# Loading x and w_ada ahead of the states' matrices, and setting up the states behind the first norm

## The chip, the cores and the metric

The kernel runs on one core of a Trainium2 chip. The metric is the device time of one execution in microseconds, the median of several runs. A core has five engines with instruction queues of their own: TensorE (PE, matrix products into eight PSUM banks), VectorE (DVE), ScalarE (ACT), GpSimd (POOL) and SyncE (SP, which here only issues DMA transfers). They wait for each other through semaphores.

## The reference, cut to what matters

One block of a hybrid model is followed by a second one of another kind; 512 tokens, 1024 features, float32. Only the beginning of the first block matters here:

```python
c_act = silu(c)
mod = c_act @ w_ada + b_ada              # six parts of 1024 columns: sh1, sc1, g1, sh2, sc2, g2
h = standardize(x) * (1 + sc1) + sh1     # the first norm
proj = h @ w_in + b_in                   # split into xm, om, ip, fp, us, ga, gb
xc = silu(causal_dwconv(xm))             # then q, k of the mLSTM heads, and v = xm
ys = gelu(s5_ssm(us, ...))               # 32 groups of 16 channels with 64 complex states each
```

In the state space model (the "states"), a small setup comes first: `dt = exp(log_dt)`, the decay `a = exp(lam * dt)` by magnitude, cosine and sine, and `b_bar = z * b` with complex `z = (a - 1) / lam`. The kernel handles eight tokens at a time: it needs the powers 0 to 8 of `a`, multiplied with c (`G5`) and with `b_bar` (`T5`), a Toeplitz matrix of the eight first responses, and a scan over 64 chunks.

## The kernel before, in words

**Weights.** All large products are float32 made of three passes: a weight block is loaded raw (512 KB, SyncE), ScalarE copies it, rounded, to `w_hi` (L1165), GpSimd subtracts to get the rest `w_lo` (L2369), and TensorE multiplies hi by hi, hi by lo and lo by hi. The blocks stand in one list (`STREAM`) that goes round through 3 raw slots, 3 `w_hi` and 3 `w_lo` slots. A raw slot is loaded again when `w_lo` of the block three before is made; a `w_hi` slot is written again when the product of the block three before has ended. `feature` (L620) takes a block of 128 output features: 24 matmuls of 128x512 (L614 to L616). `feature_pair` (L639) takes two blocks, tile by tile of h, so that it can start with the first tiles (L650 to L652). The order is us 0 to 3, xm 0 to 7, om 0 to 7, gate, gb 0 to 7, then the rest.

**The opening.** SyncE's queue issues in this order: four constants (`cols`, `ident`, `causal`, `iota`), six small transfers of the states' matrices b and c, x (2 MB), eight transfers of w_ada (1 MB each, two rows of 128 in each; parts 0 and 1, the shift and the scale). Ahead of the last two it waits until VectorE and TensorE have read b and c, which lie where these two land. Then come the weight blocks. VectorE makes the setup of the states, takes the row statistics of x (L1666), the root, and then multiplies the rows of w_ada with c and adds them up (`ada_add`, L1771 and L1773). TensorE takes three of the sixteen rows over itself (`first_columns`, L718: 5 and 7 of part 0, 7 of part 1), folds VectorE's sum over the partitions (`other_columns`, L724), and `ada_columns` (L1810) writes `mod`. ScalarE normalises x to `xn1` (L1181), TensorE turns it to eight feature tiles (`turn_h1`, L707), and ScalarE and VectorE make `h_hi` and `h_lo` out of each (`modulated`, L1200 and L1204; `modulated_low`, L1779 and L1661). A product can't start before these.

**PSUM banks.** `take` (L592) goes round a ring of banks; a bank has to be free before TensorE writes it, and TensorE's queue waits for that in order. In the opening the ring is `[4, 5, 6, 1, 2, 3, 0, 7]`: c's two transpositions take 4 and 5, part 0 takes 6, tiles 0 to 2 of h take 1, 2, 3, part 1 takes 0, and tiles 3 to 7 take 7, 4, 5, 6 and 4. The last one waits for `h_lo` of tile 4.

**The states beside the blocks.** Behind the first norm VectorE makes `G5` (L1915 to L1925, `times_powers`), the padded b (`pads`, L1931 and L1935), `T5`, and the phases of the tables (L1938 to L1946). TensorE's part stands between blocks, by a list (n counts xm 0 to 7 and om 0 to 7):

```python
s5_after = {2: [s5_kernel], 4: [lambda: s5_turn(0), lambda: s5_turn(1)], 6: [s5_inputs], 12: [s5_outputs]}
```

`s5_kernel` (L770) needs `G5` and the pads, `s5_turn` (L782) transposes each half of `T5` when it is set, `s5_inputs` (L787) needs the turned `T5` and us, `s5_outputs` (L801) needs the scans. ScalarE has a list of its own with the same steps: behind the turns it makes sine tables from the phases (L1250), behind the outputs it copies them and issues eight transfers to DRAM (L1260), and it has SiLU for the convolution of xm (`conv_out`, L1262). GpSimd sets the Toeplitz matrix to zero (L2377) behind `w_lo` of us 3.

Of the kernel before, what the change touches and what calls it, by code (L numbers as in the profile page):

```python
# [12 lines left out]
P = 128  # L13
# [142 lines left out]
def build(nc, io, out):  # L156
    with ExitStack() as ctx:
# [86 lines left out]
        T5 = [part(flat_xc, 2048 * i, NST, LC, S5G) for i in range(2)]  # L244
        ada_place = [(0, 2 * i, part(buf, 2 * (i % 2) * D, 2, D)) for i, buf in enumerate((flat_xc, flat_xc, flat_xm, flat_xm))]
        ada_place += [(1, 2 * i, part(buf, at + 2 * (i % 2) * D, 2, D)) for i, (buf, at) in enumerate(((usys, 0), (usys, 0), (s5a, 8704), (s5a, 8704)))]

        ADA_PE = ((5, 7), (7,))
# [229 lines left out]
        const_in = signal("const_in", 4, 16)  # L478
        s5_in = signal("s5_in", 6, 16)
# [3 lines left out]
        x_in = signal("x_in", 1, 16)  # L483
# [226 lines left out]
        def first_columns(part_):  # L710
# [3 lines left out]
            for kk in ADA_PE[part_]:  # L714
                n = 4 * part_ + kk // 2
                pe.wait_ge(*ada_in[n].all)
                for f in range(KD):
                    te.matmul(ps[:, f:f + 1], ada_place[n][2][:, kk % 2, f * P:(f + 1) * P], c_act[:, kk:kk + 1], start=(kk == ADA_PE[part_][0] and f == 0), stop=False)  # L718
# [21 lines left out]
        def tensor():  # L740
            pe.wait_ge(*const_in.all)
            pe.wait_ge(*s5_in.all)
            ring["misc"], turn["misc"] = [4, 5, 6, 1, 2, 3, 0, 7], 7
            for i in range(2):
                transpose(("c5", i), [c_nat[i][:, J, :, :].rearrange("p a b -> p (a b)") for J in range(4)], c_turned[2 * i + 1])
# [74 lines left out]
            s5_after = {2: [s5_kernel], 4: [lambda: s5_turn(0), lambda: s5_turn(1)], 6: [s5_inputs], 12: [s5_outputs]}  # L820
# [389 lines left out]
        def scalar():  # L1210
# [1326 lines left out]
```

## Time and profile before

| | |
|---|---|
| median of 3 runs | 1668.94 us (1664.17 to 1670.81) |
| the profiled execution | 1668.08 us, its span 1666.3 us |
| TensorE busy | 1598.5 us (96%) |
| VectorE, ScalarE, GpSimd busy | 768.3, 611.9, 618.3 us |
| first product of a weight block | at 52.03 us |

The profile page has the busy time of each engine and the chain of work that ended last, followed back from the last instruction. Its timeline lists instructions by start and duration; an entry with a count merges several. A bracket tells how long the engine sat idle before, and what released it. Overlap of a few tenths between neighbouring instructions of one engine is pipelining.

### The profile page before, as it was taken

The page shows a single profiled execution, that of the slowest core. Times are in us where ns is not written, and L with a number is a line of the kernel's source. Part 1 is how long each engine was busy: PE and PEld are TensorE (multiplying, and loading weights), DVE is VectorE, ACT ScalarE, POOL GpSimd, SP SyncE. Part 2 cuts the span into 40 slices and gives each one's busy share as a digit, 9 for nine tenths or more (in the row PEclk, how much of TensorE's full clock was granted, in tenths as well). Part 3 has the DMA queues.
Part 4 walks back from the last instruction along what each step waited for, and adds up shares of the span by engine and source line. Part 5 has one row for each costly group of instructions (what it writes and reads, how often), then busy time and mean ns, then how long its engine had stood idle before and what let it go on. Part 6 is the DMA issues. An engine that isn't in the chain of part 4 may idle for free.

```text
span 1666.3 us, 18583 instructions
## 1 busy us (share of the span) xinstructions
PE 1598.5 (96%) x7532; PEld 1298.5 (78%) x7532; DVE 768.3 (46%) x1344; ACT 611.9 (37%) x887; POOL 618.3 (37%) x266
## 2 busy tenths in 40 slices
PE   4899999989998999999999999999999999999998
PEld 4788867778887888878887888678877788888886
DVE  7879223556667444123306799751441621012103
ACT  3443464343425333123322434582442343124312
POOL 0443222224344444444454464003323344444442
PEclk9999999999999999999999999999999999999999
DMA  9393431238634354333332432002212233233322
GB/s 318 96 152 110 114 95 46 69 114 288 228 108 132 109 147 146 95 88 90 101 114 88 146 102 89 26 1 76 77 51 76 84 106 101 89 89 101 101 89 76
DMA packets 221669, 180.26 MB, mean 108 GB/s; under 512 B 24200, under 2 KB 184328, under 8 KB 221456
## 3 DMA queue, kind: packets, MB, share of 16 engines
q1 hardware_dynamic: 212368, 166.48, 34.6%
q10 hardware_dynamic: 9216, 12.60, 2.4%
q8 instruction: 59, 0.97, 0.2%
q14 instruction: 26, 0.21, 0.0%
HBM read 172.49 MB, written 6.55 MB: 107 GB/s over the span
## 4 chain that ended last, share of the span: by engine, by line
PE 78%; DVE 11%; ACT 3%; POOL 2%; issue 2%; DMA 2%; ACTq 0%; SPq 0%; DVEq 0%; POOLq 0%
PE bank L614 14%; PE bank L615 14%; PE bank L616 14%; PE bank L671 7%; PE bank L669 7%; PE bank L670 7%; DVE bank L2197 5%; PE bank L707 2%; POOL w_lo L2369 2%; DMA raw<-in_w_in 1%; PE bank L1041 1%; PE bank L1012 1%; PE bank L908 1%; PE bank L691 1%; PE bank L1098 1%
## 5 line engine op out<-in xcount | busy, mean ns | idle before, releaser
L2369 POOL TENSOR_TENSOR w_lo<-raw,w_hi 128x1024 fp32r<-128x1024 f32 (+1 forms) x246 | 595.5, 2425 | 1003.4 <-ACT w_hi L1165 1003.1
L1165 ACT ACTIVATE w_hi<-raw 128x1024 fp32r<-128x1024 f32 (+1 forms) x246 | 257.7, 1050 | 350.0 <-PE bank L671 276.6
L614 PE MATMUL bank<-h_hi,w_hi 128*128 128x512 f32 x936 | 369.8, 395 | 8.2 <-POOL w_lo L2369 6.1
L615 PE MATMUL bank<-h_lo,w_hi 128*128 128x512 f32 x936 | 366.7, 392 | 0.0
L616 PE MATMUL bank<-h_hi,w_lo 128*128 128x512 f32 x936 | 366.7, 392 | 0.0
L614 PEld LDWEIGHTS bank<-h_hi,w_hi 128*128 128x128 f32 x936 | 177.2, 189 | 50.6 <-issue 8.7
L616 PEld LDWEIGHTS bank<-h_hi,w_lo 128*128 128x128 f32 x936 | 177.0, 189 | 37.3
L615 PEld LDWEIGHTS bank<-h_lo,w_hi 128*128 128x128 f32 x936 | 177.1, 189 | 37.0 <-issue 0.7
L2197 DVE SCALAR_TENSOR_TENSOR bank<-att_area,cols,bank 128x512 f32<-128x512 f32 x116 | 87.6, 755 | 3.9
L671 PE MATMUL bank<-w_hi,u_lo 128*128 128x512 f32 x224 | 88.6, 396 | 0.0
L670 PE MATMUL bank<-w_lo,u_hi 128*128 128x512 f32 x224 | 88.6, 396 | 0.0
L669 PE MATMUL bank<-w_hi,u_hi 128*128 128x512 f32 x224 | 88.6, 396 | 0.0
L1734 DVE SCALAR_TENSOR_TENSOR x_tok<-bank,sm,x_tok 128x512 f32<-128x512 f32 x16 | 12.0, 749 | 154.9 <-PE bank L671 81.6
L2322 DVE TENSOR_TENSOR rel<-rel 128x512 f32<-128x512 f32 x32 | 30.7, 958 | 95.7 <-ACT rel L1638 95.7
L1753 DVE TENSOR_TENSOR bank<-bank,grow 128x512 f32<-128x512 f32 x24 | 16.6, 692 | 106.3 <-PE bank L693 54.3
L669 PE MATMUL bank<-w_hi,h_hi 128*128 128x512 f32 x160 | 63.8, 399 | 0.0
L671 PE MATMUL bank<-w_hi,h_lo 128*128 128x512 f32 x160 | 63.1, 394 | 0.0
L670 PE MATMUL bank<-w_lo,h_hi 128*128 128x512 f32 x160 | 62.8, 393 | 0.0
L671 PE MATMUL bank<-w_hi,act_lo 128*128 128x512 f32 x136 | 53.8, 396 | 0.0
L670 PE MATMUL bank<-w_lo,act_hi 128*128 128x512 f32 x136 | 53.8, 396 | 0.0
L669 PE MATMUL bank<-w_hi,act_hi 128*128 128x512 f32 x136 | 53.8, 396 | 0.0
L2143 DVE TENSOR_SCALAR cv_t<-tmp_f,cols 128x512 f32<-128x512 f32 x22 | 14.1, 640 | 82.7 <-ACT tmp_f L1476 82.7
(429 smaller groups left out, 2686.3 us busy)
## 6 DMA issues: line engine op xcount, KB each, us to landing
raw<-in_w_in SPq DMA_DIRECT2D x57, 512.0 KB, 4.0
raw<-in_w_ffn_up SPq DMA_DIRECT2D x44, 512.0 KB, 3.8
raw<-in_w_up SPq DMA_DIRECT2D x32, 512.0 KB, 4.0
raw<-in_w_down SPq DMA_DIRECT2D x32, 512.0 KB, 3.8
ada_ring<-in_w_ada SPq DMA_DIRECT2D x24, 512.0 KB, 5.6
raw<-in_w_ffn_down SPq DMA_DIRECT2D x20, 512.0 KB, 3.7
raw<-in_w_s_glu SPq DMA_DIRECT2D x16, 256.0 KB, 3.0
raw<-in_w_mlstm_down SPq DMA_DIRECT2D x8, 512.0 KB, 5.9
```

The lines of the kernel that those rows point to most:

```text
L614: te.matmul(ps, wv[0][:, i, :], rh, start=(i == 0), stop=False)
L615: te.matmul(ps, wv[0][:, i, :], rl, start=False, stop=False)
L616: last = te.matmul(ps, wv[1][:, i, :], rh, start=False, stop=(i == kt - 1))
L669: te.matmul(bank[b][:, :], ah, wv[0][:, i, :], start=first, stop=False)
L670: te.matmul(bank[b][:, :], ah, wv[1][:, i, :], start=False, stop=False)
L671: last = te.matmul(bank[b][:, :], al, wv[0][:, i, :], start=False, stop=final)
L691: te.matmul(bank[b][:, :], ah, wv[0][:, i, :], start=False, stop=False)
L707: last = te.transpose(ps[0:s_.shape[1], i * P:i * P + s_.shape[0]], s_, ident[0:s_.shape[0], 0:s_.shape[0]])
L1165: sc.activation(W_HI[SLOT[key]][:, 0:n], raw[:, RAW_SLOT[key], 0:n], ACT.Copy).then_inc(*hi_set.up(key))
L2197: dve.settle().scalar_tensor_tensor(acc, upad[:, f, j:j + S], w_, acc, ALU.mult, ALU.add).then_inc(*dve.step())
L2322: ve.tensor_tensor(sq, rl, rl, ALU.mult).then_inc(*u_sq.up(m))
L2369: gp_.tensor_tensor(W_LO[s_][:, 0:n], raw[:, RAW_SLOT[key], 0:n], W_HI[s_][:, 0:n].bitcast(F32), ALU.subtract).then_inc(*lo_made.up(key))
```

## The change

SyncE issues x behind three constants, in two halves, then w_ada, then three weight blocks; the states' matrices and `causal` follow once part 1's columns are folded. w_ada goes in nine transfers, the last two of one row of 128 each, and TensorE's own rows are now 1 and 3 of part 0 and 1 of part 1. VectorE starts with the norm, and the setup of the states stands behind `modulated_low`; ScalarE's exponent and sine for it stand behind `modulated`. TensorE transposes c behind the first pair of blocks. The ring of banks is another one. `s5_kernel`, `s5_turn` and `s5_inputs` come two blocks later, `s5_outputs` one, and the wait for the Toeplitz matrix's transfers with them; GpSimd's memset comes behind xm 3.

```diff
-        ada_place += [(1, 2 * i, part(buf, at + 2 * (i % 2) * D, 2, D)) for i, (buf, at) in enumerate(((usys, 0), (usys, 0), (s5a, 8704), (s5a, 8704)))]
-        ADA_PE = ((5, 7), (7,))
+        ada_place += [(1, 2 * i, part(buf, at, 2, D)) for i, (buf, at) in enumerate(((usys, 0), (usys, 2 * D), (s5a, 8704)))]
+        ada_place += [(1, 6 + i, part(s5a, 8704 + (2 + i) * D, 1, D)) for i in range(2)]
+        ADA_PE = ((1, 3), (1,))
...
         def tensor():
             pe.wait_ge(*const_in.all)
-            pe.wait_ge(*s5_in.all)
-            ring["misc"], turn["misc"] = [4, 5, 6, 1, 2, 3, 0, 7], 7
-            for i in range(2):
-                transpose(("c5", i), [c_nat[i][:, J, :, :].rearrange("p a b -> p (a b)") for J in range(4)], c_turned[2 * i + 1])
+            ring["misc"], turn["misc"] = [4, 1, 2, 5, 6, 3, 0, 7], 7
...
             first_columns(0)
+            for f in range(4):
+                turn_h1(f)
             other_columns(0)
-            for f in range(3):
-                turn_h1(f)
             first_columns(1)
-            turn_h1(3)
+            turn_h1(4)
             other_columns(1)
-            for f in range(4, 7):
-                turn_h1(f)
-            turn["misc"] = 7
+            turn_h1(5)
+            turn_h1(6)
+            turn["misc"] = 4
             turn_h1(7)
...
             feature_pair([("us", 0), ("us", 1)], h_hi, h_lo, h1_ready, [us_out[0], us_out[1]])
+            pe.wait_ge(*s5_in.all)
+            for i in range(2):
+                transpose(("c5", i), [c_nat[i][:, J, :, :].rearrange("p a b -> p (a b)") for J in range(4)], c_turned[2 * i + 1])
...
-            s5_after = {2: [s5_kernel], 4: [lambda: s5_turn(0), lambda: s5_turn(1)], 6: [s5_inputs], 12: [s5_outputs]}
+            s5_after = {4: [s5_kernel], 6: [lambda: s5_turn(0), lambda: s5_turn(1)], 8: [s5_inputs], 13: [s5_outputs]}
...
         def scalar():
-            act.wait_ge(*s5_dve["pow"])
-            sc.activation(E9, E9, ACT.Exp).then_inc(*s5_act.up("pow"))
-            act.wait_ge(*s5_dve["cs"])
-            sc.activation(pw5[:, 0:288], pw5[:, 288:576], ACT.Sin, scale=SIN_SCALE).then_inc(*s5_act.up("cs"))
...
                 modulated("h1", f, mod[:, KD + f:KD + f + 1], mod[:, f:f + 1], h1_sv, h1_dv, h1_hi)
+            act.wait_ge(*s5_dve["pow"])
+            sc.activation(E9, E9, ACT.Exp).then_inc(*s5_act.up("pow"))
+            act.wait_ge(*s5_dve["cs"])
+            sc.activation(pw5[:, 0:288], pw5[:, 288:576], ACT.Sin, scale=SIN_SCALE).then_inc(*s5_act.up("cs"))
...
-            s5_after = {2: [s5_kernel], 4: [lambda: s5_turn(0), lambda: s5_turn(1), s5_tables], 9: [lambda: conv_out(0, 2)], 12: [s5_outputs], 13: [lambda: conv_out(2, 4)], 14: [lambda: conv_out(4, 6)], 15: [lambda: conv_out(6, 8)]}
+            s5_after = {4: [s5_kernel], 6: [lambda: s5_turn(0), lambda: s5_turn(1), s5_tables], 10: [lambda: conv_out(0, 2)], 13: [s5_outputs, lambda: conv_out(2, 4)], 14: [lambda: conv_out(4, 6)], 15: [lambda: conv_out(6, 8)]}
...
         def vector():
+            for i in range(2):
+                dve.wait_ge(*x_in[i].all)
+                row_stats(2 * i, 2, x_tok)
+            row_variance("x", 0, TT, 0, LN_EPS, False)
+            row_inverse("x", 0, TT, 0, shift=True)
+            dve.wait_ge(*c_set.all)
+            for p_ in range(2):
+                for kk in ada_dve(p_):
+                    n, rows_ = ada_rows_at[p_, kk]
+                    ada_add(p_, kk, rows_, ada_in[n].all)
+                    if (p_, kk) == (1, 6):
+                        ada_columns(0, 0, 0.0)
+            ada_columns(1, KD, 1.0)
+            dve.wait_ge(*mod_set[1])
+            for f in range(0, KD, 2):
+                modulated_low("h1", f, KD, 0, h1_dv, h1_hi, h1_lo)
...
             dve.wait_ge(*turned["h1", KD - 1])
+            dve.wait_ge(*c_turned[3])
             times_powers(G5, c5, LC + 1, -1, g5_set)
...
         def gpsimd():
             gp_.memset(ones[:, :], 1.0).then_inc(*ones_set.up())
-            pool_low_to(INDEX["us", 3])
-            pool.wait_ge(*ada_sum[1])
-            pool.wait_ge(*ada_col[1])
+            pool_low_to(INDEX["xm", 3])
+            pool.wait_ge(*b5_set.all)
+            pool.wait_ge(*turned["c5", 1])
             gp_.memset(toep, 0.0).then_inc(*toep_zero.up())
...
         def sync():
+            def s5_matrices():
+
+                sp.wait_ge(*ada_col[1])
+                for i, nm in enumerate(("s5_b_re", "s5_b_im")):
+                    sy.dma_start((b_re, b_im)[i], io[nm][0].rearrange("g p c -> (g p) c").rearrange("(j p) c -> p j c", p=P)).then_inc(*s5_in.up(i))
+                for i, nm in enumerate(("s5_c_re", "s5_c_im")):
+                    for d_ in range(2):
+                        sy.dma_start(c_nat[i][:, :, d_, :], io[nm][0].rearrange("g c p -> (g c) p").rearrange("(j p) s -> p j s", p=P)).then_inc(*s5_in.up(2 + 2 * i + d_))
+                sy.dma_start(causal[:, :], io["causal"]).then_inc(*s5_in.up(6))
...
+            for i in range(2):
+                sy.dma_start(x_tok[:, 2 * i:2 * i + 2, :], io["x"][0, 2 * i * P:2 * (i + 1) * P].rearrange("(t p) d -> p t d", p=P)).then_inc(*x_in[i].up())
             for n, (p_, k0, place_) in enumerate(ada_place):
-                if n == len(ada_place) - 2:
-                    sp.wait_ge(*turned["c5", 1])
-                    sp.wait_ge(*b5_set.all)
...
             for r_, (key, parts) in enumerate(STREAM):
+                if r_ == NRAW:
+                    s5_matrices()
...
-                if key == ("om", 0):
+                if key == ("om", 2):
                     sp.wait_ge(*k_rows_out.all)
                     sp.wait_ge(*toep_zero.all)
```

## Rows read from the trace of the kernel before

**Rows 1.** The page: TensorE's busy time, and the chain that ended last.
```profile
PE 1598.5 (96%) x7532; PEld 1298.5 (78%) x7532; DVE 768.3 (46%) x1344; ACT 611.9 (37%) x887; POOL 618.3 (37%) x266
...
PE 78%; DVE 11%; ACT 3%; POOL 2%; issue 2%; DMA 2%; ACTq 0%; SPq 0%; DVEq 0%; POOLq 0%
```

**Rows 2.** TensorE's waits, 0 to 330 us: us in total, times, longest.
```profile
PE bank L718 <- DMA xmT<-in_w_ada: 12.5, 1, 12.5
PE bank L707 <- DMA s5a<-in_s_c_im: 9.8, 1, 9.8
PE bank L707 <- DVE h_lo L1661: 3.7, 1, 3.7
PE bank L614 <- POOL w_lo L2369: 3.3, 3, 1.9
```

**Rows 3.** Timeline, 0 to 56 us: start, duration, engine, line, operation.
```profile
2.59 0.43 SPq L2403 DMA_DIRECT2D s5a<-in_s_b_re  x1
...
6.30 0.18 DVE L1829 TENSOR_TENSOR s5a<-cols,s5a 128x16 f32<-128x16 f32 x1 [1.38 <-ACT s5a L1213]
...
7.20 0.51 SPq L2407 DMA_DIRECT2D x_tok<-in_x  x1
...
14.97 1.77 DVE L1887 COPY s5a<-bank 64x256 f32<-64x256 f32 x4
...
16.77 4.85 DVE L1666 BATCH_NORM_STATS2 stats<-x_tok 128x6 f32<-128x512 f32 x8
...
38.73 1.27 DVE L1773 SCALAR_TENSOR_TENSOR scr<-s5a,sm,scr 128x1024 f32<-128x1024 f32 x1
38.82 1.06 ACT L1165 ACTIVATE w_hi<-raw 128x1024 fp32r<-128x1024 f32 x1 [10.42 <-DMA raw<-in_w_in]
...
41.46 3.41 PE L724 MATMUL bank<-ones,scr 128*128 128x1 f32 x16
...
44.91 0.17 DVE L1810 SCALAR_TENSOR_TENSOR mod<-bank,cols 128x8 f32<-128x8 f32 x1 [4.91 <-PE bank L724]
...
46.52 1.29 DVE L1661 SCALAR_TENSOR_TENSOR h_lo<-bank,h_hi 128x512 fp32r<-128x512 f32 x2 [0.59 <-ACT h_hi L1204]
...
51.26 1.12 PE L707 MATMUL bank<-ident,s5a 128*128 128x128 f32 x4 [3.73 <-DVE h_lo L1661]
...
52.03 0.78 PE L650 MATMUL bank<-h_hi,w_hi 128*128 128x512 f32 x1
```

**Rows 4.** The tile x_tok: its transfer.
```profile
DMA to landing us min/median/max: 9.2/9.2/9.2
```

**Rows 5.** A stretch: busy time of each engine, granted clock, DMA share, GB/s.
```profile
10.00:20.00 10.00, 1.76 (x8) 1.36 (x7) 9.46 (x31) 1.26 (x1) 0.00 (x0) 1.00 1.02 404
```

**Rows 6.** VectorE's and GpSimd's timelines, 50 to 330 us.
```profile
80.72 4.37 DVE L1915 TENSOR_TENSOR xcT<-s5a 128x2048 f32<-128x2048 f32 x1
85.01 2.28 DVE L1918 TENSOR_TENSOR s5a<-s5a 128x2048 f32<-128x2048 f32 x1
...
67.63 4.25 POOL L2369 TENSOR_TENSOR w_lo<-raw,w_hi 128x1024 fp32r<-128x1024 f32 x1 [20.70 <-ACT w_hi L1165]
...
80.53 2.41 POOL L2369 TENSOR_TENSOR w_lo<-raw,w_hi 128x1024 fp32r<-128x1024 f32 x1 [0.31 <-ACT w_hi L1165]
...
192.49 0.96 POOL L2381 MEMSET rows<- 128x1024 f32 x1
```

**Rows 7.** The tile usys, 190 to 197 us: duration ns min/median/max, starts.
```profile
L1989 DVE SCALAR_TENSOR_TENSOR usys<-usys,cols x4: 737/738/752, 192.3 to 194.4; 128x512 f32<-128x512 f32 x4
```

**Rows 8.** The chain that ended last, in order of time.
```profile
107.59 3.49 PE bank L707 x32
...
182.84 1.07 ACT w_hi L1165
...
199.25 1.75 PE bank L707 x16
```

**Rows 9.** TensorE in stretches of 2 us: busy, granted clock, DMA.
```profile
186.00:188.00 2.00, 1.52 (x4) 0.67 0.16 40
188.00:190.00 2.00, 2.00 (x6) 0.50 0.94 300
```

More of the change, by code:

```diff
@@ L245, in build @@
         ada_place = [(0, 2 * i, part(buf, 2 * (i % 2) * D, 2, D)) for i, buf in enumerate((flat_xc, flat_xc, flat_xm, flat_xm))]
-        ada_place += [(1, 2 * i, part(buf, at + 2 * (i % 2) * D, 2, D)) for i, (buf, at) in enumerate(((usys, 0), (usys, 0), (s5a, 8704), (s5a, 8704)))]
-        ADA_PE = ((5, 7), (7,))
+        ada_place += [(1, 2 * i, part(buf, at, 2, D)) for i, (buf, at) in enumerate(((usys, 0), (usys, 2 * D), (s5a, 8704)))]
+        ada_place += [(1, 6 + i, part(s5a, 8704 + (2 + i) * D, 1, D)) for i in range(2)]
+        ada_rows_at = {(p_, k0 + i): (n, place_[:, i, :]) for n, (p_, k0, place_) in enumerate(ada_place) for i in range(place_.shape[1])}
+        ADA_PE = ((1, 3), (1,))
         ada_acc = [grow, scr[:, 0:2, :].rearrange("p a b -> p (a b)")]
@@ L477, in build @@
         TTC = [(c, t) for t in range(TT) for c in range(2)]
-        const_in = signal("const_in", 4, 16)
-        s5_in = signal("s5_in", 6, 16)
+        const_in = signal("const_in", 3, 16)
+        s5_in = signal("s5_in", 7, 16)
         us_rows_out, us_chunks_in = signal("us_rows_out", US, 16), signal("us_chunks_in", LC, 16)
@@ L482, in build @@
         ys_rows_out, ys_in = signal("ys_rows_out", LC, 16), signal("ys_in", 1, 16)
-        x_in = signal("x_in", 1, 16)
+        x_in = [signal(f"x{i}_in", 1, 16) for i in range(2)]
         ada_in = [signal(f"ada{i}_in", 1, 16) for i in range(len(ada_place))]
@@ L714, in first_columns @@
             for kk in ADA_PE[part_]:
-                n = 4 * part_ + kk // 2
+                n, rows_ = ada_rows_at[part_, kk]
                 pe.wait_ge(*ada_in[n].all)
                 for f in range(KD):
-                    te.matmul(ps[:, f:f + 1], ada_place[n][2][:, kk % 2, f * P:(f + 1) * P], c_act[:, kk:kk + 1], start=(kk == ADA_PE[part_][0] and f == 0), stop=False)
+                    te.matmul(ps[:, f:f + 1], rows_[:, f * P:(f + 1) * P], c_act[:, kk:kk + 1], start=(kk == ADA_PE[part_][0] and f == 0), stop=False)
         def other_columns(part_):
@@ L1887, in vector @@
                     ve.tensor_copy(c5[i][gs, :, :], src[gs, :, g, :]).then_inc(*c_turned.up(2 * i + g))
-            dve.wait_ge(*x_in.all)
-            row_stats(0, TT, x_tok)
-            row_variance("x", 0, TT, 0, LN_EPS, False)
-            row_inverse("x", 0, TT, 0, shift=True)
-            dve.wait_ge(*c_set.all)
-            for p_ in range(2):
-                for kk in ada_dve(p_):
-                    n = 4 * p_ + kk // 2
-                    ada_add(p_, kk, ada_place[n][2][:, kk % 2, :], ada_in[n].all)
-                    if (p_, kk) == (1, 5):
-                        ada_columns(0, 0, 0.0)
-            ada_columns(1, KD, 1.0)
-            dve.wait_ge(*mod_set[1])
-            for f in range(0, KD, 2):
-                modulated_low("h1", f, KD, 0, h1_dv, h1_hi, h1_lo)
             def times_powers(dst, x, n, signs, done):
@@ L2398, in sync @@
         def sync():
[L2399 to L2407 removed]
+            def s5_matrices():
[6 more added lines that the diff above has]
+                sy.dma_start(causal[:, :], io["causal"]).then_inc(*s5_in.up(6))
+            for i, (dst, nm) in enumerate(((cols, "cols"), (ident, "ident"))):
+                sy.dma_start(dst[:, :], io[nm]).then_inc(*const_in.up(i))
+            sy.dma_start(iota, io["iota"][:, 0:NC]).then_inc(*const_in.up(2))
+            for i in range(2):
+                sy.dma_start(x_tok[:, 2 * i:2 * i + 2, :], io["x"][0, 2 * i * P:2 * (i + 1) * P].rearrange("(t p) d -> p t d", p=P)).then_inc(*x_in[i].up())
             for n, (p_, k0, place_) in enumerate(ada_place):
[L2409 to L2411 removed]
                 rows_ = slice(k0 * P, (k0 + place_.shape[1]) * P)
```

8 lines of the change are left out of this document (removed).

## The prediction

> **What bounds the kernel now.** I read the page first. TensorE is busy for 96% of the span and holds 78% of the chain that ended last [rows 1], so what can be gained is time in which it has no matmul. Next came TensorE's own waits over the first 330 us [rows 2]: 12.5 and 9.8 us fall ahead of the first real product, 3.7 on `h_lo`, 3.3 on `w_lo`. Then I followed the timeline up to that product [rows 3]. The six transfers for the states are issued from 2.59 us, x only at 7.20. x takes 9.2 us to land [rows 4], so until 16.4. VectorE starts its statistics at 16.77 and from there has no gap until its last row of w_ada at 38.73 + 1.27 = 40.0. TensorE folds that sum (41.46 to 44.87), `mod` is set at 45.08, and the first product starts at 52.03. It could have begun when `h_lo` of tiles 0 and 1 was there, at 46.52 + 1.29 = 47.8; it stood behind the transposition of tile 7, which waited until 51.26 for the bank of tile 4. After that products follow each other, and no later wait in that list is for anything that keeps its own date (a transfer issued early, say). A start g earlier is a gain of g unless the states' work turns up late.
>
> **The first norm.** Four transfers instead of ten stand ahead of x; its first half goes out at 2.1 us. The DMA moves 404 GB/s at full rate [rows 5], 2.6 us per MB. x's 2 MB need 5.2 us, so before they began to flow at 11.2; the small packets of the states had the time ahead of it. The constants land 2.4 us after their issue, so I put x's flow at 4, its halves at 6.5 and 9.1, and the eight MB of w_ada at 11.7, 14.3, ... 27.2, 29.8. Latest case: x at 10.5. VectorE: statistics cost 4.85 / 8 = 0.61 each [rows 3], four of them behind the second half, to 11.6; variance and root take 2.0, as before, so the first row at 13.6. Rows cost 0.75 and then 1.33 each; six, then seven. They now run into the DMA: part 0 ends at 22.2, part 1 can't pass its second transfer before 24.6, and ends at 32.8. TensorE's share, columns of rows 1 and 3 and then row 1, is early. Folding takes 3.5 + 0.2: `mod` at 36.5 instead of 45.08, 8.6 earlier (7 to 9.5). ScalarE's three `w_hi` must be ahead of that: before, the first raw block was there at 38.82 [rows 3], 1.9 us behind w_ada's end, the others at 40.6 and 42.1; so now 31.7, 33.5 and 35.0, and the last copy ends at 36.1.
>
> **The banks.** Tile 7 now takes part 1's bank, free once `mod` is set. TensorE turns tiles 5 to 7 until 39.1, and `h_lo` of tile 1 is there 2.7 us after `mod`, at 39.2. `w_lo` of the second block is ready at 37.6 (the first raw block at 31.7, 1.06 for `w_hi`, twice 2.4 for `w_lo`). First product at 39.2 instead of 52.0: **12.8**. The 2.56 us per tile of the pair at its slow start (0.43 us a matmul) give VectorE the same room as before.
>
> **Added waits.** SyncE waits for part 1's columns (36.3), then issues seven transfers, 5 us; behind them stand the blocks us 3, xm 0 and xm 1, issued from 41.9 and wanted at 53.8, so nothing. The states' matrices land by 44, wanted at 52. ScalarE waits for VectorE's exponents and phases until 49.2; behind that is `w_hi` of us 3, which needs the pair's end at 52.3 anyway. Without this cover each us would be one of TensorE's.
>
> **The eight transpositions of c** leave idle time and go behind the pair: sixteen took 1.75 us at full pace [rows 8], so **-0.9**. They let GpSimd finish us 3's `w_lo` (now 56.9, wanted 58.7) and, its memset being gone from there, xm 0's. Of the 3.3 us for `w_lo` in three waits the longest, 1.9, lies at 186 [rows 2]; the other two, at these blocks, go: **+1.4** (0 to 1.6).
>
> **VectorE's chain.** This decides. It is done with `h_lo` at 36.5 + 9.4 - 0.4 = 45.5. Setup takes 14.97 - 6.30 = 8.7 (54.2), the four copies 1.8 (56.0) [rows 3], and us 3's `w_lo` holds the first product to 56.7. Then come six products by 2.52, the pads, six products by 2.28. Bare, that is 15.1 + 2.1 + 13.8 = 31.0. Before it took 54.51 to 100.7 = 46.2. The other 15.2 is GpSimd: a VectorE product that meets a `w_lo` stands still for it (4.37 at 80.72 beside 2.28 at 85.01, with the `w_lo` from 80.53 [rows 6]), or GpSimd does (4.25 at 67.63 beside 2.4) and VectorE's next one pays. A `w_lo` costs 2.15, and the memset, which met the copies, 3.5. Now nine `w_lo` (xm 0 to om 0) fall in: 56.7 + 31.0 + 19.35 = 107.0. The memset falls beside a product with two SBUF inputs. The trace has that pair once: four such at 192.35, the memset at 192.49, and none is longer than 0.75 [rows 6, 7]. So it costs 0 (bounds 0 and 3.5; 0 is the row of the same pair). The Trainium skill says so too (SBUF — State Buffer, "SBUF: two separate sides"): an operation with two SBUF inputs is locked out only by a GpSimd operation that reads SBUF. The trace agrees. By this rule the chain ends at 107.0; were a memset a lock-out for every VectorE operation, at up to 110.5, which is the first rival.
>
> When is it wanted? Before, the turns began at 107.6 [rows 8], 55.6 us after the first product. Minus 1.4, plus 0.9 and two blocks of 24 matmuls at 0.227 (5.45), that is 39.2 + 66.0 = 105.2, and the second turn, which needs the last product, 1.8 later: 107.0, just when it is there. **0** (to -6: two `w_lo` more, 4.3, and 1.8 for the clock, below). The other dates have room: pads at 87 for the states' kernel at 92.2; phases at 113.4, so ScalarE is back with om 1 at about 121, wanted at 123.4; the scans, 28 us from 123.4, end at 151.4 and are wanted from 162.
>
> **Behind the outputs.** These come one block later in order, at om 5, with two blocks made ahead as before. There ScalarE's eight issues hold the next `w_hi` until 182.84, and TensorE stands 2.1 us and then runs at a granted 0.67 and 0.50 (this is 1.2 GHz) until 190 [rows 8, 9]. Now two SiLUs stand ahead of that `w_hi` as well (1.15 in all): **-1.15**. ys rows, read 13 us behind the outputs, are wanted 21 behind.
>
> **Sum.** 12.8 - 0.9 + 1.4 + 0 - 1.15 = 12.15. The profiled execution took 1668.1 (span 1666.3 and 1.8 around it), 0.9 under the median of 1668.94. 1668.9 - 12.1 = **1656.8**; this case alone 1654 to 1660.
>
> **Rivals.** *The states' chain comes late at the second turn.* For it: the date is met without a tenth to spare. If the memset costs VectorE its 3.5 (the copies' price), the chain ends up to 3.5 behind (2.6 where it falls between products); a stop of 2.1 halved the clock before for 3.7 us, which costs 1.8. Gain 12.15 - 2.6 - 1.8 = 7.8: 1661; with a `w_lo` or two more, 1664. *The start is earlier by less.* The first blocks come behind all of w_ada; if the DMA gives the time ahead of x no use and they land at the old 38.8 and 40.6, `w_lo` of us 1 is at 44.7, the first product gains 7.3, the sum 7.3 - 0.9 + 1.4 - 1.15 = 6.7: 1662. Against it: no transfer waits for VectorE any more, where SyncE stood until 15.14. *Slower.* The same chain, far later: us for us TensorE stands at the second turn, ScalarE at the phases with om 1's `w_hi` behind it. It breaks even from an end at 119 instead of 107 and is 0.5% slower from 127; that is nine more `w_lo` at 2.15, twice those I count. A change of 20 us would give 1677. *No effect*, 1669: only if a later stage waits on something that doesn't move; the chain shows none.
>
> **How the numbers follow.** Forecast 0.54, late chain 0.22, smaller start 0.12, slower 0.06, no effect 0.06. 0.5%, or 8.3 us, is about what a measurement can tell from no change; that line, 1660.6, leaves the forecast faster, and a third of the first two rivals. Faster 0.54 + 0.11, same 0.23 + 0.06, slower 0.06. Range 1653.5 to 1664: it takes in the forecast and most of the two partial gains.
>
> **What would show it.** `mod`'s second column at 36.5 and the first product at 39.2; no stop at us 3; the last of VectorE's second six at 107 and the memset beside one of the first six without a product of 5 us; a stop below 1 us at the second turn; a stop of about 3 us ahead of the gate block. Wrong would be a first product after 42, or TensorE idle over 2 us between 104 and 112.

## The result, and the profile after

The changed kernel takes **1657.25 us** (median of 8 runs, 1651.01 to 1661.47), the kernel before, beside it on the same chip, 1666.56 (8 runs, 1660.78 to 1672.71; the 3 runs of the forecast's 1668.94 are among them): a ratio of 0.9942 with a 95% interval of 0.9914 to 0.997. A later repetition gave 1657.29 against 1665.87, 0.9944 (0.9924 to 0.9964). It is faster by 0.6%, 9 us, where 12.1 were forecast and 1656.8 was named. The profiled execution took 1659.67 (span 1657.9) against 1668.08 (span 1666.3).

The page of the changed kernel, and its TensorE's waits from 0 to 330 us, which answer to [rows 1, 2]:

```profile
PE 1591.4 (96%) x7532; PEld 1292.8 (78%) x7532; DVE 778.4 (47%) x1344; ACT 613.2 (37%) x887; POOL 626.4 (38%) x266
```
```profile
PE bank L721 <- DMA xcT<-in_w_ada: 12.8, 1, 12.8
PE bank L727 <- DVE scr L1776: 5.6, 1, 5.6
PE bank L710 <- ACT s5a L1247: 4.6, 1, 4.6
...
PE bank L617 <- POOL w_lo L2374: 1.9, 1, 1.9
PE bank L853 <- ACT v_tok L1302: 1.6, 1, 1.6
...
PE bank L653 <- DVE h_lo L1664: 0.5, 1, 0.5
```

Gone are the 9.8 for c and the 3.7 for `h_lo`, and of the three stops for `w_lo` two. New is 4.6 for `s5a`: the second turn, for which VectorE's chain of products came too late. The line 1.6 for `v_tok`, ahead of the first product of q and k, is new too.

The opening, from the timeline of the changed kernel, 0 to 56 us, against [rows 3]:

```profile
2.12 0.94 SPq L2418 DMA_DIRECT2D x_tok<-in_x  x2
...
7.27 2.47 DVE L1669 BATCH_NORM_STATS2 stats<-x_tok 128x6 f32<-128x512 f32 x4 [2.55 <-DMA x_tok<-in_x]
10.12 2.47 DVE L1669 BATCH_NORM_STATS2 stats<-x_tok 128x6 f32<-128x512 f32 x4 [0.38 <-DMA x_tok<-in_x]
...
25.50 2.61 DVE L1776 SCALAR_TENSOR_TENSOR scr<-usys,sm,scr 128x1024 f32<-128x1024 f32 x2 [1.70 <-DMA usys<-in_w_ada]
...
32.31 1.28 DVE L1776 SCALAR_TENSOR_TENSOR scr<-s5a,sm,scr 128x1024 f32<-128x1024 f32 x1
32.53 1.06 ACT L1168 ACTIVATE w_hi<-raw 128x1024 fp32r<-128x1024 f32 x1 [13.16 <-DMA raw<-in_w_in]
33.65 3.57 PE L727 MATMUL bank<-ones,scr 128*128 128x1 f32 x16 [5.61 <-DVE scr L1776]
37.26 0.17 DVE L1813 SCALAR_TENSOR_TENSOR mod<-bank,cols 128x8 f32<-128x8 f32 x1 [3.67 <-PE bank L727]
40.42 0.47 PE L653 MATMUL bank<-h_hi,w_hi 128*128 128x512 f32 x1 [0.54 <-DVE h_lo L1664]
```

VectorE now starts 9.5 us sooner and waits for rows of w_ada on the way (1.70 in one place). Part 1's sum ends at 33.6, `mod` is set at 37.4, the first product starts at 40.42: 11.6 earlier than 52.03.

VectorE's chain, its timeline over the same kernel, against [rows 6]:

```profile
53.88 2.52 DVE L1900 TENSOR_TENSOR s5a<-s5a 128x256 f32<-128x256 f32 x1
56.32 2.63 DVE L1901 TENSOR_TENSOR s5a<-s5a 128x256 f32<-128x256 f32 x1
58.98 0.42 DVE L1902 TENSOR_TENSOR s5a<-s5a 128x256 f32<-128x256 f32 x1
61.13 4.37 DVE L1919 TENSOR_TENSOR s5a<-s5a 128x2304 f32<-128x2304 f32 x1
...
77.24 2.55 DVE L1922 TENSOR_TENSOR s5a<-s5a 128x2304 f32<-128x2304 f32 x1
...
106.92 2.29 DVE L1927 TENSOR_TENSOR xcT<-xcT,s5a 128x2048 f32<-128x2048 f32 x1
```

And GpSimd's timeline beside it:

```profile
53.70 2.41 POOL L2374 TENSOR_TENSOR w_lo<-raw,w_hi 128x1024 fp32r<-128x1024 f32 x1 [13.05 <-ACT w_hi L1168]
56.26 2.40 POOL L2374 TENSOR_TENSOR w_lo<-raw,w_hi 128x1024 fp32r<-128x1024 f32 x1 [0.15 <-ACT w_hi L1168]
...
74.84 3.53 POOL L2382 MEMSET s5a<- 128x4096 f32 x1
```

The reader is to see two things. A product of 0.42 us (58.98) takes 2.52 and 2.63 where it meets a `w_lo` of 2.4: what a meeting costs doesn't depend on how short VectorE's operation is. And the product at 77.24 takes its bare 2.55 with the memset (until 78.37) beside its first 1.1 us. The six products start at 61.13 instead of 56.7, and the last of the second six ends at 109.2 instead of 107.0.

TensorE's timeline where the turns are, and its stretches of 2 us there (busy, granted clock, DMA, GB/s):

```profile
103.46 1.91 PE L710 MATMUL bank<-ident,xcT 128*128 128x128 f32 x16
109.99 3.65 PE L710 MATMUL bank<-ident,xcT 128*128 128x128 f32 x16 [4.62 <-ACT s5a L1247]
```
```profile
110.00:112.00 2.00, 2.00 (x10) 0.50 1.60 88
112.00:114.00 2.00, 2.00 (x10) 0.50 1.43 136
114.00:116.00 2.00, 2.00 (x8) 0.66 1.15 293
116.00:118.00 2.00, 2.00 (x11) 1.00 0.48 118
```

TensorE is ready for the second turn 4.62 us early; after that stop it runs at a granted 0.50 (1.2 GHz) for over 4 us, and the sixteen transpositions take 3.65 instead of 1.91.

Behind the outputs, ScalarE's timeline, against the `w_hi` in [rows 8]:

```profile
180.81 1.05 ACT L1168 ACTIVATE w_hi<-raw 128x1024 fp32r<-128x1024 f32 x1
191.06 1.06 ACT L1168 ACTIVATE w_hi<-raw 128x1024 fp32r<-128x1024 f32 x1 [3.94 <-DMA raw<-in_w_in]
192.03 0.57 ACT L1294 ACTIVATE rows<-bank 8x512 f32<-8x512 f32 x1
```

The gate's rows were there to be copied at about 190, but ScalarE's order has a `w_hi` ahead of them whose raw block lands only at 191.

ScalarE's eight issues for the outputs, before and after, and then TensorE (busy, granted clock, DMA, GB/s) behind the stop for `w_lo` that follows the outputs, in the first profile and in e11, a second execution of the same kernel:

```profile
174.58 8.21 ACTq L1260 DMA_DIRECT2D ys_rows<-s5a  x8
...
172.55 7.15 ACTq L1263 DMA_DIRECT2D ys_rows<-s5a  x8
```
```profile
184.43 0.47 PE L617 MATMUL bank<-h_hi,w_hi 128*128 128x512 f32 x1 [1.94 <-POOL w_lo L2374]
...
184.00:186.00 2.00, 1.57 (x7) 1.00 0.71 227
186.00:188.00 2.00, 2.00 (x11) 1.00 1.05 399
```
```profile
181.80 0.47 PE L617 MATMUL bank<-h_hi,w_hi 128*128 128x512 f32 x1 [1.92 <-POOL w_lo L2374]
...
182.00:184.00 2.00, 2.00 (x7) 0.68 0.90 349
184.00:186.00 2.00, 2.00 (x6) 0.50 1.04 366
```

The stop is as long in both, but only in e11 does the granted clock fall behind it: the block of 24 matmuls there takes 7.17 us up to the next transposition instead of 5.57. So 1.6 us of any difference at the first product of q and k can be this clock and not an edit.

One more table belongs here, since several readings hang on it. **[e11] below is the same kernel in another execution.** The places of four landmarks in all profiles ("pair" is from the start of its first matmul to that of its last; the outputs come one block, 5.4 us, later in the order than before, in every kernel made from the changed one but the one in the fourth row, where it is two):

| kernel | first product | pair | stop at second turn | outputs end | first q, k product | median us |
|---|---|---|---|---|---|---|
| before | 52.03 | 13.1 | none | 173.44 | 213.51 | 1666.6 |
| after | 40.42 | 10.8 | 4.62 | 171.40 | 206.22 | 1657.25 |
| after, again (e11) | 41.20 | 13.1 | 1.37 | 168.79 | 203.72 | 1657.29 |
| e3, turns later | 41.24 | 10.9 | 1.26 | 171.93 | 206.12 | 1657.91 |
| e1, bank alone | 48.04 | 12.0 | none | 169.16 | 206.84 | 1663.46 |
| e2, order alone | 44.38 | 12.7 | 1.33 | 171.51 | 206.26 | 1659.81 |
| e4, low parts later | 40.80 | 12.8 | 1.42 | 168.15 | 203.00 | 1656.88 |
| e5, memset twice | 40.56 | 10.7 | 3.92 | 171.08 | 206.27 | 1662.81 (one run) |
| e6, small first | 45.95 | 13.0 | 1.34 | 173.40 | 207.95 | 1662.61 |
| e7, gate rows first | 41.23 | 12.5 | 1.34 | 168.18 | 203.88 | 1656.15 |
| e9 = e4 + e7 | 40.65 | 12.5 | 1.44 | 167.75 | 201.32 | 1653.92 |
| e8 = e9 + turns later | 40.94 | 12.8 | none | 166.76 | 200.67 | 1653.18 |
| e8 again (e10) | 40.66 | 12.7 | none | 166.31 | 200.27 | 1652.99 |

Whole runs of one kernel spread over 8 to 17 us, so the landmarks carry the finer readings, and medians only the sums. The landmarks move too: e11, e4, e7 and e9 differ in nothing that acted up to the outputs (see e4), and their outputs end within 1.0 us of each other. Counted from the pair's last matmul it is 114.5 to 114.6 us in all four, and in e2 and e6 as well. From the stop behind the outputs to the next transposition it is 5.54 to 5.57 us at full pace (after, e5, e8, e9, e10) and 7.14 to 7.17 behind a halved clock (e2, e4, e6, e7, e11).

### The profile page after: what moved, and what is told of

Its sections match the earlier page's. It is cut to its first block, busy times and chain, and to the rows that moved or that the text cites. A ratio compares the mean times of both kernels' runs of the same rounds, so it can differ in the third digit from the quotient of the medians.

```text
span 1657.9 us, 18585 instructions
## 1 busy us (share of the span) xinstructions
PE 1591.4 (96%) x7532; PEld 1292.8 (78%) x7532; DVE 778.4 (47%) x1344; ACT 613.2 (37%) x887; POOL 626.4 (38%) x266
## 4 chain that ended last, share of the span: by engine, by line
PE 58%; DVE 10%; ACT 2%; POOL 1%; issue 1%; DMA 0%; DVEq 0%; ACTq 0%
PE bank L617 9%; PE bank L618 9%; PE bank L619 9%; PE bank L672 7%; PE bank L674 7%; PE bank L673 7%; DVE bank L2202 5%; PE bank L710 2%; PE bank L1044 1%; PE bank L1015 1%; POOL w_lo L2374 1%; PE bank L694 1%; PE bank L1101 1%; PE bank L695 1%; PE bank L696 1%
## 5 line engine op out<-in xcount | busy, mean ns | idle before, releaser
L2374 POOL TENSOR_TENSOR w_lo<-raw,w_hi 128x1024 fp32r<-128x1024 f32 (+1 forms) x246 | 603.6, 2458 | 981.8 <-ACT w_hi L1168 981.7
```

The costliest lines, as they stand in the source:

```text
L2374: gp_.tensor_tensor(W_LO[s_][:, 0:n], raw[:, RAW_SLOT[key], 0:n], W_HI[s_][:, 0:n].bitcast(F32), ALU.subtract).then_inc(*lo_made.up(key))
```

## The experiments

Medians are of 6 to 12 runs; the kernel before, beside them, had 1666.75 (e1 to e4), 1665.2 (e5 to e8) and 1665.87 (e9 to e11).

**e1_bank_only.** The kernel before, with only the bank of tile 7 changed.
```diff
-            turn["misc"] = 7
+            turn["misc"] = 5
             turn_h1(7)
```


> The kernel before with one edit: tile 7 of h takes part 1's bank (free once mod is set) instead of the bank of tile 4. Theory (the start passes through): in the kernel before the second turn had some 7 us of room behind T5 (set at 100.7, turns from 107.6), so the first product starts at about 48 instead of 52 and the gate block about 4 us earlier; the time falls by 4. If TensorE also keeps or loses full pace at the pair because the 3.7 us without a matmul are gone, the pair takes 10.9 instead of 13.1 us and the gain is 6. Rival (the opening's gain is swallowed later): no change of the gate's start.


Measured 1663.46, ratio 0.999 (0.9972 to 1.0008). The first product starts 4.0 us earlier, as the term of the sum has it, the outputs end 4.3 earlier. The time's interval takes in no change, so that the bank is paid for in time isn't shown; the landmarks show it up to the outputs.

**e2_old_bank_wait.** The changed kernel, tile 7 waiting again for the bank of an earlier tile: the order's part by itself.
```diff
-            turn["misc"] = 4
+            turn["misc"] = 5
             turn_h1(7)
```


> The changed kernel with tile 7 put back behind h_lo of tile 4 by its bank (bank 0). The first product should start about 3.5 us later than in the changed kernel (40.4 to about 44). Theory A (VectorE's chain sets the date of the second turn): TensorE stopped 4.6 us there, so it stops about 1 us now, T5 is set at the same 109, and the whole time stays within 1 us of the changed kernel. Rival B (each us of start is a us of the end): 3.5 us slower than the changed kernel. If the pace of the pair depends on the gap ahead of it, its 48 matmuls take more than 11 us.


Measured 1659.81, ratio 0.9962 (0.9943 to 0.9982). Against the first profile of the changed kernel the start is 4.0 later and outputs and q, k are where they were, which looks as if VectorE's chain set the date alone. Against e11, whose pair ran at a like pace, start, outputs' end and q, k are 3.2, 2.7 and 2.5 later. The medians differ by 2.5, the gains over the kernel before by 1.6 (6.9 against 8.6), and the intervals of the two ratios overlap. VectorE's chain is later too (last product 111.8 against 109.0), since it meets other `w_lo`. So by the landmarks most of a later start is paid, and that reading of mine fell with e11. At q, k the bank seems worth 6.7 us in the old order (213.51 to 206.84) and 2.5 in the new (206.26 to 203.72). But 1.6 of the 6.7 is the clock behind the outputs (12.61 us from stop to transposition before, 10.99 in e1) and 0.8 a shorter stop there (1.95 and 1.18); 4.3 is what the bank and a quicker pair gave up to the outputs.

**e3_turns_later.** Both turns one block later, inputs and outputs too.
```diff
-            s5_after = {4: [s5_kernel], 6: [lambda: s5_turn(0), lambda: s5_turn(1)], 8: [s5_inputs], 13: [s5_outputs]}
+            s5_after = {4: [s5_kernel], 7: [lambda: s5_turn(0), lambda: s5_turn(1)], 9: [s5_inputs], 14: [s5_outputs]}
```
(ScalarE's list likewise, its tables at 7, its columns of xc at 11, 14 and 15.)


> The changed kernel with the turns, the inputs and the outputs of the states one block later again (turns behind xm 7, inputs behind om 1, outputs behind om 6). Theory A (the 4.6 us stop at the second turn and the halved clock behind it, together about 6 to 7 us, are the price of the late chain): the stop shrinks to under 1 us and the gate block starts 5 to 7 us earlier than in the changed kernel, minus up to 1 us if ScalarE is back late; total 4 to 6 below the changed kernel. Rival B: the wait moves on to the phases and w_hi of om 2, and nothing is won.


Measured 1657.91, ratio 0.996 (0.994 to 0.9979): nothing won. The stop at the second turn falls to 1.26; behind the outputs a new one of 2.7 for `v_tok` stands at the transpositions, and that ahead of q, k grows from 1.6 to 2.4: with the outputs a block later, what follows them has a block less to hide behind. This reason is argued from the order; only the stops are shown.

**e4_low_behind_b.** GpSimd makes us 3's `w_lo` and the next ones only behind VectorE's short products.
```diff
-            pool_low_to(INDEX["xm", 3])
+            pool_low_to(INDEX["us", 2])
             pool.wait_ge(*b5_set.all)
+            pool_low_to(INDEX["xm", 3])
```


> The changed kernel with one more wait: GpSimd makes w_lo of us 3 and xm 0 only when VectorE has set b_bar (two products with 256 columns that stood still for 4.4 us beside these two w_lo). Theory A (the lock-out of VectorE by w_lo is why its chain was 4.4 us later than forecast at its start): b_bar is set at about 55 instead of 59.4, the chain starts at 57 and T5 is set about 3 to 4 us earlier (105 to 106 instead of 109.2); the stop at the second turn shrinks by as much, while TensorE may stop up to 1 us at us 3. Net 2 to 3 us below the changed kernel. Rival B: VectorE's products are slow for another reason (their operands land late), and only TensorE's wait at us 3 is added.


Measured 1656.88, ratio 0.9947 (0.9929 to 0.9965). The chain starts at 57.19 and ends at 108.4, against 61.13 and 109.2 in the first profile of the changed kernel. But this execution's pair took 12.8, and with such a pair the unedited kernel has the short products bare too (e11). Beside that one it is 0.6 to 0.7 earlier, at the chain's end and at q, k, but its start is 0.4 earlier as well, and e7, which lacks the wait, ends its chain at 108.5 and its outputs at 168.18. The wait held nothing here: the short products ended at 55.45, and the first of these `w_lo` began at 56.17, released by its `w_hi`; it is the same in e8, e9 and e10 (55.75 to 56.32). What the wait is worth when the pair takes 10.8 no run shows.

**e5_memset_twice.** The memset of the Toeplitz tile done twice, one run.
```diff
-            gp_.memset(toep, 0.0).then_inc(*toep_zero.up())
+            gp_.memset(toep, 0.0).then_inc(*pool.step())
+            pool.settle().memset(toep, 0.0).then_inc(*toep_zero.up())
```


> The changed kernel with GpSimd's memset of the Toeplitz matrix made twice (the same zeros again), to read what a memset costs VectorE's products. Theory A (a memset doesn't lock out an operation with two SBUF inputs): the two memsets, 7 us, run beside the products of the first six, and a product that starts with them takes its bare 2.55 us; the first six end within 1 us of the changed kernel (84.5). Rival B (every GpSimd operation locks VectorE out): two products take 6 us and more and the first six end 3.5 us later. w_lo of xm 4 comes 3.5 us later in either case and TensorE may stop for it.


VectorE's and then GpSimd's timeline of this kernel:
```profile
72.70 4.75 DVE L1919 TENSOR_TENSOR s5a<-s5a 128x2304 f32<-128x2304 f32 x1
77.37 2.55 DVE L1922 TENSOR_TENSOR s5a<-s5a 128x2304 f32<-128x2304 f32 x1
79.95 2.56 DVE L1929 SCALAR_TENSOR_TENSOR s5a<-s5a 128x2304 f32<-128x2304 f32 x1
```
```profile
74.97 3.53 POOL L2382 MEMSET s5a<- 128x4096 f32 x1
78.56 3.53 POOL L2383 MEMSET s5a<- 128x4096 f32 x1
```
Two memsets of 3.53 lie beside two-input products that take their bare 2.55, and neither memset is held. The stop at the second turn got shorter, not longer: xm 4's `w_lo` came later, and the first six products ended at 82.5 instead of 84.5. The single run, 1662.81, is 1.3 us above the highest of the changed kernel's 17, but q, k began at 206.27, as without the second memset (206.22): the difference lies behind it.

**e6_small_first.** The six transfers of b and c (to an unused place) ahead of x again, all else as changed.
```diff
+            for i, nm in enumerate(("s5_b_re", "s5_b_im")):
+                sy.dma_start(part(s5a, 12800 + 256 * i, NST, S5G), ...).then_inc(*extra_in.up(i))
...
             for i in range(2):
```


> The changed kernel with six more transfers ahead of x: the states' b and c once more, into a place that nothing reads (VectorE waits for them only ahead of its tables). This measures what the six small transfers cost the opening. Theory (they hold the DMA queues and push back all behind them by their own time): x's halves land 5 to 7 us later than at 7.3 and 10.1, the last row of w_ada too, mod is set at 42 to 44 instead of 37.4, and the first product starts at 45 to 47. By the forecast, which put the effect of the order of the loads at 7.3 us for x, it would be 47. The whole time then is 4 to 7 us over the changed kernel, since VectorE's chain starts later by as much. Rival (VectorE's sums are the limit, not the DMA): the first product is less than 3 us later.


Its timeline's opening:
```profile
13.11 5.02 DVE L1670 BATCH_NORM_STATS2 stats<-x_tok 128x6 f32<-128x512 f32 x8 [8.29 <-DMA x_tok<-in_x]
...
37.84 1.28 DVE L1777 SCALAR_TENSOR_TENSOR scr<-s5a,sm,scr 128x1024 f32<-128x1024 f32 x1
```
Last row and `mod` come 5.5 us later (32.31 to 37.84, 37.26 to 42.79), the first product too (45.95). Measured 1662.61, ratio 0.9985 (0.9971 to 0.9998): 5.4 over the changed kernel's first median; the gain over the kernel before beside it is 2.6, where the changed kernel's was 9.3.

**e7_gate_rows_first.** ScalarE copies and sends the gate's rows ahead of the next `w_hi`.
```diff
-            high_ahead("gate", 0)
             act.wait_ge(*gemm["gate", 0])
...
+            high_ahead("gate", 0)
             act.wait_ge(*v_ones.all)
```


> The changed kernel with one line moved in ScalarE's order: the gate's rows are copied (and their DMA issued) ahead of w_hi of gb 1, not behind it. In the changed kernel ScalarE waited 3.9 us for gb 1's raw block, and the rows were copied at 192.03 although the gate block had ended at 190.0; the first product of q and k came 14.2 us behind the rows, in the kernel before 14.2 as well. Theory A (this wait is one of the two places where the opening's gain was given back): rows at 190.1, q and k at 204.3 instead of 206.2; total about 2 below the changed kernel, hard to tell by the times. Rival B (q and k wait for something else): 206 as before.


ScalarE's timeline:
```profile
188.79 0.59 ACT L1293 ACTIVATE rows<-bank 8x512 f32<-8x512 f32 x1 [4.69 <-PE bank L619]
...
190.64 1.06 ACT L1168 ACTIVATE w_hi<-raw 128x1024 fp32r<-128x1024 f32 x1 [1.26 <-issue]
```
The rows now follow their product, but q, k doesn't start earlier than in e11 (203.88 against 203.72), where the old order had them at 189.51. The trace has two reasons. Here too the clock was halved behind the outputs, so the gate's product ended only at 188.6 and the old order would hardly have held its rows (by 0.5 us in e11). And the `w_hi` that came first now stands between the rows and `v_tok`, for which TensorE stops ahead of q, k: from the transposition behind the gate's product to q, k it is 15.3 us in e7 to e10, 14.7 in e11 and e4 (old order, halved clock) and 16.2 in the first profile (old order, full pace). So the edit gives 0.9 us at full pace and costs 0.6 behind a halved clock. Measured 1656.15, ratio 0.9947 (0.9926 to 0.9968): by itself within the changed kernel's spread.

**e8_all_three.** e4 and e7, and the turns and inputs one block later with the outputs left at 13.
```diff
-            s5_after = {4: [s5_kernel], 6: [lambda: s5_turn(0), lambda: s5_turn(1)], 8: [s5_inputs], 13: [s5_outputs]}
+            s5_after = {4: [s5_kernel], 7: [lambda: s5_turn(0), lambda: s5_turn(1)], 9: [s5_inputs], 13: [s5_outputs]}
```


> The changed kernel with three edits: GpSimd's w_lo of us 3 and xm 0 behind b_bar, the states' turns and inputs one block later (7 and 9; the outputs stay at 13), and the gate's rows ahead of w_hi of gb 1. Theory A: no stop at the second turn (T5 is set at 108, wanted at 111), so no halved clock behind it, outputs end at about 166 (171.4 in the changed kernel), q and k begin at 199 to 200 (206.2); total 5 to 7 us below the changed kernel. Rival B (the scans, now 4 us later in the order, are late for the outputs, wanted from 150): a wait inside the outputs eats the gain.


Measured **1653.18**, ratio 0.993 (0.9909 to 0.9952). No stop at either turn, q, k at 200.67, with full pace behind the outputs.

**e9_b_and_gate.** e4 and e7 alone; the turns as in the changed kernel.


> The changed kernel with two of the three repairs: GpSimd holds its low parts of us 3 back until b_bar is set, and ScalarE copies the gate's rows ahead of the next high part; the states' turns stay where the changed kernel has them. Theory (both stops are paid by TensorE, each by itself): chain of VectorE starts at about 57, last product ends at 108.4, a stop of 1.3 us stays at the second turn, the gate's rows follow its block at once, first q,k product at 203.0 - 2.0 = 201 to 202, time 1 to 2 us over the version with all three. Rival (the moved turns gave nothing, as when they were moved alone): same time as with all three, first q,k product at 200.7 or below. Second rival (what is won up to q,k is given back later): no better than the changed kernel, 1657.


Measured 1653.92, ratio 0.993 (0.9905 to 0.9955); a stop of 1.44 stays, q, k at 201.32, in the place that the theory gave. Two steps that gave 0.4 and 1.1 us alone gave 3.4 against the changed kernel beside them (e11), and 2.4 at q, k. At q, k this is luck in the main: 1.6 of the 2.4 is the clock, which stayed at 1.00 behind the outputs in e9 and fell to 0.50 in e11, 1.0 came before the outputs' end (an earlier start by 0.55, a quicker pair by 0.6), and a 0.3 shorter stop is set against the 0.5 that the moved `w_hi` costs; e4's wait again held nothing. What sets the clock, and how much of the medians' 3.4 is the edits', isn't settled.

**e10_all_again.** The version of e8 once more.


> The version with all three repairs once more, in more rounds and beside the other two of this call. If its lead is real, 1653 again, 3 to 5 us below the changed kernel in the same call, and 12 below the kernel before. If it was the spread of 10 us that each kernel has from run to run, 1656 to 1658.


Measured 1652.99, ratio 0.9922 (0.9898 to 0.9945): the lead of 4.3 over the changed kernel repeats. TensorE's turns in it, one row for both:
```profile
111.04 3.83 PE L710 MATMUL bank<-ident,xcT 128*128 128x128 f32 x32
```
Moving the turns gave 1.05 at q, k against e9 (201.32 to 200.27, with full pace behind the outputs in both), and from the pair's last matmul to the outputs' end 113.0 us in e8 and e10 instead of 114.6; the medians, 0.9 apart, can't tell that.

**e11_after_again.** The changed kernel, nothing edited.


> The changed kernel itself, nothing edited, as the measure for the other two on the same chip: 1657 (1651 to 1661), ratio to before 0.994. Its profile is a second look at the opening: first product at 40.4 in either case; if the pair's pace differs between executions of one kernel, the pair may take up to 13 us in place of 10.8, the two-input products of b_bar then run free of w_lo, and the stop at the second turn is 1.3 us in place of 4.6, with the outputs' end where it was.


Measured 1657.29, ratio 0.9944 (0.9924 to 0.9964). VectorE's timeline, and TensorE's turns:
```profile
54.66 0.43 DVE L1900 TENSOR_TENSOR s5a<-s5a 128x256 f32<-128x256 f32 x1
...
57.60 4.07 DVE L1919 TENSOR_TENSOR s5a<-s5a 128x2304 f32<-128x2304 f32 x1
```
```profile
106.60 1.91 PE L710 MATMUL bank<-ident,xcT 128*128 128x128 f32 x16
109.88 2.03 PE L710 MATMUL bank<-ident,xcT 128*128 128x128 f32 x16 [1.37 <-ACT s5a L1247]
```
The pair took 2.3 us more than in the first profile, and q, k came 2.5 **earlier**. The slower pair frees the slot for us 3's `w_hi` later, so us 3's `w_lo` begins behind the short products (56.84) instead of among them (53.70), the chain starts 3.5 earlier, and the stop at the turn is too short to halve the clock. The expectation had the outputs' end unmoved; it moved by 2.6. The same two patterns divide the other profiles of this opening: pair near 10.8, chain from 61.1 to 62.0 (after, e3, e5); pair of 12.5 or more, chain from 57.0 to 57.6 (e4, e7 to e11).

## Why the forecast came out, step by step

**The opening, 12.8: right in place, 11.6 and 10.8 measured.** x's halves were there at 7.3 and 10.1 instead of 6.5 and 9.1. Part 1 ended at 33.6 and 34.4 instead of 32.8, and `mod` was set at 37.4 and 38.2 instead of 36.5; the last 0.3 fell behind it. The two parts of the term are borne out one by one: the bank 4.0 by e1 (4.2 forecast), the six small transfers 5.5 of the 7.7 at `mod` by e6. The remaining 2.2 belong to the rest of the new order (VectorE's setup behind the norm, x in halves, SyncE without its waits), which wasn't taken apart; the opening itself moves by 0.8 between executions (37.4 and 38.2 for `mod`). "Four transfers instead of ten" are three, by the change and the timeline; the issue of x at 2.1 is right. The rival of a late raw block is out: the first `w_hi` starts at 32.53, where 31.7 was forecast and 38.8 feared.

**c's transpositions and the stops of `w_lo`, -0.9 and +1.4: right.** The eight lie at full pace between the pair and us 2; of three stops for `w_lo` one is left.

**The memset, 0: right, and shown by doubling it (e5).** The Trainium skill (SBUF — State Buffer, "SBUF: two separate sides") has a two-input VectorE operation locked out only by a GpSimd operation that reads SBUF. The traces agree: 2.55 beside a memset, 4.64 to 4.75 beside a `w_lo`. In the same section the Trainium skill has the lock held for the whole instruction, and the 0.42 us products that take 2.5 and 2.6 agree with that as well.

**VectorE's chain: the step that was mis-sized.** "Setup takes 14.97 - 6.30 = 8.7 (54.2), the four copies 1.8 (56.0)" counts no `w_lo` there. With a pair of 10.8 two fall in, the chain starts at 61.1 and ends at 109.2; with a pair of 13.1 none does, and it runs from 57.6 to 109.0. Either way it is 2 us late. In the first profile that is 4.4 at the start, less a `w_lo`: within the twelve products and the pads GpSimd took 17.1 us (48.1 less the bare 31.0), eight meetings, where 19.35, nine, were forecast. In e11 it is 0.9 at the start, since `mod` and with it the setup came late, and 20.4 us in ten meetings. So both have ten `w_lo` from the setup to the end, one more than the forecast. Us 3's `w_lo`, which was to hold the first product to 56.7, did so in neither. And "**0** (to -6)" for the second turn was in truth -1.4 (e11) to -7.4 (the first profile): 4.62 of waiting, 3.65 - 1.91 = 1.7 for the transpositions, and 5 matmuls 0.43 apart instead of 0.227, 1.0. The late chain, the rival that had 0.22, is thus what the first profile shows, and larger than it was priced (2.6 + 1.8 = 4.4), not for the memset but for the "`w_lo` or two more" that it had as an addition. "TensorE idle over 2 us between 104 and 112" was named as what would make the forecast wrong, and in one of two profiles it was so; "a stop below 1 us at the second turn" was so in neither.

**Behind the outputs, -1.15: too dear by 0.9.** From the outputs' end to q, k, with the block of 5.45 counted that now lies ahead of the outputs, the change cost 0.2 us in the first profile and 0.3 in e11. The stop was forecast at 3.3 us with a halved clock behind it, as before [rows 8, 9]. It was 1.94 and 1.92, as before (1.95): two SiLUs of 1.15 do stand ahead of that `w_hi`, but the eight issues ahead of them took 7.15 us instead of 8.21. The halved clock behind it came in e11 and not in the first profile. What the first profile saved by that was given back in a stretch that no step had: ScalarE's order holds the gate's rows behind a `w_hi` whose raw block lands late, 192.03 instead of about 190, and TensorE then stands 1.6 (0.2 in e11) ahead of q, k. That block is issued behind the 1 MB of the states' outputs (182.42); that this delays it is likely and wasn't tested.

**The sum.** Up to the outputs' end, a block of 5.45 added: forecast 12.8 - 0.9 + 1.4 = 13.3; measured 173.44 - 168.79 + 5.45 = 10.1 in e11 (the terms above give 10.8 - 0.9 + 1.4 - 1.4 = 9.9) and 7.5 in the first profile (11.6 - 0.9 + 1.4 - 7.4, and 2.3 for the faster pair, 7.0). Up to q, k: forecast 12.15; measured 9.8 and 7.3. Behind that the three profiles are alike (1452.8 us of span before, 1451.7 and 1451.8 after), which is in part chance: in the others the same stretch takes 1444.8 (e7) to 1461.5 us (e1), and it is there that most of the spread between runs lies. The medians' 9.3 and 8.6 lie between. So 1656.8 against 1657.25 is closer than its terms: the kernel before was at 1668.94 when the forecast was made and at 1666.56 beside the changed one, and that 2.4 hides that the gain was 3 us too large.

**Where the rest went** is shown in part by e8 and its repetition: 12.0 and 12.9 us under the kernel before, about what the forecast had for the change alone, once the chain is no longer late for its turn. Up to the outputs' end they gained 12.1 and 12.6 where 13.3 were forecast, and what is missing lies in the start, which came 1.7 and 1.4 us later than forecast. Behind it they gained 0.7 where the forecast had a loss of 1.15, and there the full clock of these executions gave 1.6, which can't be put down to the edits.

## What to carry to other kernels

A chain that is due "without a tenth to spare" is not a zero in the sum: price the case in which it is late, with the halved clock behind the stop, and leave it a block of room if the stage behind has room too (e8 and e10 kept the outputs in place and ended them 1.6 us sooner behind the pair than e9; e3 moved them too, and gained nothing). Where two engines lock each other out, count the meetings in the short operations as well, since each costs the long one's length. And two profiles of one kernel are worth more than a finer reading of one: the first made an experiment look decided that the second undid. Compare the granted clock behind each stop before a difference of 2 us between two profiles is put down to an edit; and an added wait is tested only if the trace shows that something waited for it.

## What the runs showed of the hardware

**The pace of the pair.** The same program's first 48 matmuls took 10.8 us in some executions and 12.5 to 13.1 in others. In e11, as before, the record grants 1.00 over the whole opening, while the first dozen matmuls behind the start come 0.43 us apart, the pace that the first profile shows from 113.86 to 115.14 at a granted 0.50 (1.2 GHz). It is so in e1, e2, e4, e6 and e8 too (six to eleven slow matmuls): there the granted clock in the record and the pace part. In the other six profiles (the first, e3, e5, e7, e9, e10) they agree. In the first profile the record shows 0.50 from 28 to 40 us, 0.93 at 40 to 42 and 1.00 behind it, and the matmuls come 0.23 apart from the second on:
```profile
38.00:40.00 2.00, 1.88 (x9) 0.50 0.80 85
40.00:42.00 2.00, 1.58 (x7) 0.93 0.84 116
```
What TensorE did before divides the two groups: in these six it took 1.95 to 2.3 us for part 0's folding, from 23 to 24 us on, the record falls to 0.50 between 26.5 and 27.8 us, while it still works, and it then stands 5.4 to 5.6 us ahead of the last folding; in the others that first folding took 3.57, and the stop was 2.5 (none before and in e1). The record then rises to 1.00 between 40 and 42 us in three of the six (the first, e3, e5; pair near 10.8) and between 44 and 46 in the other three (e7, e9, e10; pair 12.5 to 12.7). What sets these dates no run here tells. So a granted 1.00 in an opening doesn't prove full pace; the distance of the matmuls does.

**A stop of 2 us can halve the clock or not.** Behind the outputs TensorE stood 1.85 to 2.17 us in e2, e4, e6, e7, e11 and the kernel before, and then ran at a granted 0.50 for some us, which cost 1.6; it stood 1.94 to 2.18 us in the first profile, e5, e8 and e10, and 1.63 in e9, and stayed at 1.00. The length of the stop doesn't divide them. The stops of 1.26 to 1.44 us at the second turn (seven profiles) cost only themselves, those of 4.62 and 3.92 (the first profile and e5) had the halved clock behind them.
